# A mixture-of-experts layer behind an attention block: experts' outputs scaled on leaving PSUM and summed in DRAM by accumulating scatters, the tail's weights streamed as a 33rd expert

## The reference

```
xt = rms_norm(h, ffn_norm)
top_vals, top_idx = top_k(xt @ w_router + b_router, 4); gates = softmax(top_vals)
for expert e, for its tokens:
  y = ((clip(xt @ w_up[e] + b_up[e]) + 1) * swish(min(xt @ w_gate[e] + b_gate[e], 7))) @ w_down[e] + b_down[e]
h = h + sum over a token's 4 experts of gate * y
gate = sigmoid(rms_norm(h, ple_gate_norm) @ w_ple_gate)          # 1024 x 1024
e    = rms_norm(p @ w_ple_proj, ple_post_norm)                   # p: 512 x 256
h    = h + gate * e
```

## Time and profile before

| | |
|---|---|
| median of 3 runs | 2425.62 us |
| the profiled execution | 2424.97 us, its span 2423.1 us |
| mean granted clock of TensorE | 0.932 |
| PE, DVE, ACT, POOL busy | 90%, 65%, 55%, 10% |
| first product of the first expert | at 1137.2 us |
| last product of the last expert | done at 2290.5 us |
| tail | 2290.5 to 2423.1 us |

### The profile page before, as it was taken

The page is one execution under the profiler, slowest core; times in us unless marked ns, Lnnn a source line. Parts: engine busy times, 40 slices in busy tenths (PEclk is TensorE's granted clock), DMA queues, the critical chain, the costliest instruction groups (busy, mean ns, idle before and its releaser), DMA issues.

```text
span 2423.1 us, 31445 instructions
## 1 busy us (share of the span) xinstructions
PE 2171.8 (90%) x10638; PEld 1792.3 (74%) x10638; DVE 1564.7 (65%) x1788; ACT 1333.8 (55%) x1692; POOL 232.9 (10%) x168
## 2 busy tenths in 40 slices
PE   4985797899989597986999999999999999999828
PEld 3874675788868586775888888888888888888617
DVE  3314772222232436557988988988898898898753
ACT  2213452222222423314888888888888888888722
POOL 0000000000000000002111211211221121121220
PEclk9987798999999897697999999999999999999969
DMA  3334002122322221032999999999999999999850
GB/s 132 105 140 155 30 1 78 61 100 92 104 70 87 96 70 57 1 116 108 404 377 381 383 374 380 378 384 381 378 381 380 377 384 377 378 384 378 331 199 35
DMA packets 91167, 546.88 MB, mean 226 GB/s; under 512 B 13317, under 2 KB 15961, under 8 KB 32986
## 3 DMA queue, kind: packets, MB, share of 16 engines
q1 hardware_dynamic: 71744, 493.90, 54.1%
q10 hardware_dynamic: 12154, 25.84, 2.9%
q0 software_dynamic: 7200, 26.22, 2.7%
HBM read 514.98 MB, written 29.36 MB: 225 GB/s over the span
## 4 chain that ended last, share of the span: by engine, by line
PE 86%; DVE 7%; DMA 2%; ACT 2%; issue 2%; ACTq 0%; POOL 0%; POOLq 0%; DVEq 0%; SPq 0%
PE PS L1953 15%; PE PS L1955 14%; PE PS L1954 14%; PE PS L233 10%; PE PS L235 10%; PE PS L234 10%; PE PS L1950 2%; PE PS L922 2%; PE PS L307 2%; PE PS L1871 1%; PE PS L1963 1%; PE PS L1351 1%; DMA RING<-c_oh 1%; PE PS L990 1%; DVE X L2252 1%
## 5 line engine op out<-in xcount | busy, mean ns | idle before, releaser
L1865 DVE TENSOR_TENSOR WL<-RING,WH 128x2048 fp32r<-128x2048 f32 x388 | 879.5, 2287 | 111.1 <-ACT WH L1861 107.7
L1861 ACT ACTIVATE WH<-RING 128x1024 fp32r<-128x1024 f32 x776 | 807.9, 1058 | 174.8 <-PE PS L1955 165.5
L1953 PE MATMUL PS<-WH,RA 128*128 128x512 f32 x1540 | 639.1, 415 | 0.0
L1955 PE MATMUL PS<-WH,RA 128*128 128x512 f32 x1540 | 600.9, 390 | 0.0
L1954 PE MATMUL PS<-WL,RA 128*128 128x512 f32 x1540 | 600.2, 390 | 0.0
L229 DVE TENSOR_TENSOR WL<-RING,WH 128x2048 fp32r<-128x2048 f32 (+2 forms) x60 | 133.4, 2224 | 480.6 <-ACT WH L221 480.6
L221 ACT ACTIVATE WH<-RING 128x2048 fp32r<-128x2048 f32 (+2 forms) x60 | 111.6, 1860 | 477.3 <-PE PS L235 445.9
L1955 PEld LDWEIGHTS PS<-WH,RA 128*128 128x128 f32 x1540 | 289.4, 188 | 62.8
L1954 PEld LDWEIGHTS PS<-WL,RA 128*128 128x128 f32 x1540 | 290.1, 188 | 58.9
L1953 PEld LDWEIGHTS PS<-WH,RA 128*128 128x128 f32 x1540 | 291.2, 189 | 54.5
L233 PE MATMUL PS<-WH,RA 128*128 128x512 f32 (+2 forms) x640 | 246.1, 385 | 45.3 <-DVE RA L322 30.8
(11 more groups left out here) (330 smaller groups left out, 2285.0 us busy)
## 6 DMA issues: line engine op xcount, KB each, us to landing
RING<-w_experts SPq DMA_DIRECT2D x390, 1024.0 KB, 7.2
RING<-w_front SPq DMA_DIRECT2D x60, 1024.0 KB, 4.9
y_scr<-AR ACTq DMA_DIRECT2D x32, 512.0 KB, 8.9
y_scr<-AR SPq DMA_DIRECT2D x16, 512.0 KB, 5.1
RING<-w_tail SPq DMA_DIRECT2D x4, 1024.0 KB, 6.4
X<-x SPq DMA_DIRECT2D x4, 512.0 KB, 5.6
xs_scr<-AR ACTq DMA_DIRECT2D x4, 512.0 KB, 3.4
out<-X SPq DMA_DIRECT2D x4, 512.0 KB, 2.6
```

The source lines that it names most:

```text
L1861: e.activation(WH[:, m % 3, v], RING[:, m % 6, v], ACT.Copy).then_inc(s("m_hi"), 1)
L1865: e.tensor_tensor(WL[:, m % 3, :], RING[:, m % 6, :], WH[:, m % 3, :].bitcast(F32), ALU.subtract).then_inc(s("m_lo"), 1)
L1953: e.matmul(PS[bank][:, :], lhs[0][:, kr + k, :], WH[:, m % 3, c], start=False, stop=False)
L1955: x = e.matmul(PS[bank][:, :], lhs[1][:, kr + k, :], WH[:, m % 3, c], start=False, stop=(stop and k == 3))
```

## The change

1. **Lists.** Empty slots now name token 768, and gathers and scatters run with a bounds check of 511, which leaves such rows out. A second list, `GLIST`, holds each slot's gate. It is made by the same kind of matmul, with the gates cut into three bfloat16 parts (`GB`) and multiplied into the one-hot matrices by POOL (`OHG`, `BLM`: six multiplications). The 32 list matmuls (16 for `GLIST`, 16 for the overflow blocks) move from the end of the routing to behind the first expert's first product (`pe_late_lists`).
2. **Order.** The splits of the first expert's pieces 1 and 2 move on ACT and DVE from behind the routing to within it. `SLOTN` moves behind the low part of the first expert's rows (`XL`).
3. **Experts.** ACT scales by the column `GCOL` while it copies from PSUM; `YY` is added into `acc_scr` (a copy of `X` in DRAM, stored by SP during the routing) by an indirect DMA from POOL's queue that accumulates. POOL copies the two columns for it (`GCOL`, `TCOL`) once the scatter before has landed; ACT waits for them.
4. **Tail.** `w_experts` has a 33rd expert with the tail's weights, which the last expert's prefetch loads; three of its pieces are also split within the loop. `g_moe` is raised twice, first without the wait for the last scatter. `X` is read back from `acc_scr`, the gathers and the 16 additions are gone. TensorE transposes `X` unscaled, in 32 transposes, and the scale is applied in the sigmoid; the result is stored in eight halves.
5. `y_scr`, its filling with zeros and the waits for it are gone.

The DMA of `c_iot` into `RE4` only raises `d_y` to its first 16. The core of the diff:

```diff
-            e.wait_ge(s("v_win"), AT["v_gm"] + 8)
-            e.memset(ZERO, 0.0).then_inc(s("g_zero"), 1)
-
-        def sp_zero(e):
-            e.wait_ge(s("g_zero"), 1)
-            for b in range(NOV):
-                e.dma_start(y_d[(NE + b) * 128:(NE + b + 1) * 128, :], ZERO).then_inc(s("d_zero"), 16)
...
                 sp_expert_load(e, n, n, 0)
+
+            for i in range(4):
+                e.wait_ge(s("v_x"), 20 + i + 1)
+                e.dma_start(acc_d[i * 128:(i + 1) * 128, :], X[:, i, :]).then_inc(s("d_acc"), 16)
...
+
+        def pe_late_lists(e):
+
             for i in range(4):
                 for k in range(4):
-                    x = e.matmul(PS[3][:, 128:144], SLOTN[:, i, k, :], BLO[:, i, k, :], start=(i == 0 and k == 0),
+                    if i == 0 and k == 0:
+                        e.wait_ge(s("g_ohg"), 3)
+                    x = e.matmul(PS[4][:, 0:96], SLOT1[i][:, k, :], OHG[:, 4 * i + k, :, :], start=(i == 0 and k == 0), stop=(i == 3 and k == 3))
+            x.then_inc(s("p_rt"), 1)
+            e.wait_ge(s("v_route"), AT["v_blm"] + 1)
+            e.wait_ge(s("g_blm"), 3)
+            for i in range(4):
+                e.wait_ge(s("v_slot"), i + 1)
+                for k in range(4):
+                    x = e.matmul(PS[5][:, 0:80], SLOTN[:, i, k, :], BLM[:, i, k, :, :], start=(i == 0 and k == 0),
                                  stop=(i == 3 and k == 3))
             x.then_inc(s("p_rt"), 1)
 
...
+            e.wait_ge(s("p_pr"), CH[62].done)
+            act_expert_split(e, 1, 16, None)
             rows_put(0, 0, 0)
...
+            e.wait_ge(s("p_pr"), CH[63].done)
+            act_expert_split(e, 2, 16, None)
             for i in range(4):
...
             places(0)
+            dve_expert_split(e, 1, 4)
             best(2)
             places(1)
+            dve_expert_split(e, 2, 6)
...
-            e.tensor_scalar(LIST[:, 0:32], PS[7][:, 0:32], 256.0, None, ALU.add).then_inc(s("v_route"), 1)
+
+            e.tensor_scalar(LTMP, PS[7][:, 32:64], -512.0, 768.0, ALU.mult, ALU.add).then_inc(v_c.sem, v_c.up())
+            e.wait_ge(v_c.sem, v_c.n)
+            e.tensor_tensor(LIST[:, 0:32], LTMP, PS[7][:, 0:32], ALU.add).then_inc(s("v_route"), 1)
...
+            e.tensor_copy(GB[:, 0, :], fl(GK)).then_inc(v_c.sem, v_c.up())
+            e.wait_ge(v_c.sem, v_c.n)
+            e.tensor_tensor(GR1, fl(GK), GB[:, 0, :], ALU.subtract).then_inc(v_c.sem, v_c.up())
+            e.wait_ge(v_c.sem, v_c.n)
+            e.tensor_copy(GB[:, 1, :], GR1).then_inc(v_c.sem, v_c.up())
+            e.wait_ge(v_c.sem, v_c.n)
+            e.tensor_tensor(GB[:, 2, :], GR1, GB[:, 1, :], ALU.subtract).then_inc(s("v_route"), 1)
             dve_steps(e, QK, POSK, TMK, (128.0, 256.0, 384.0)).then_inc(v_c.sem, v_c.up())
...
-                e.tensor_tensor(BLT, mid(IOT16, 4), bc(TMK[:, i, :], 16), ALU.is_equal).then_inc(v_c.sem, v_c.up())
...
-                x = e.tensor_tensor(SLOTN[:, i], mid(IOT, 4), bc(PMK[:, i, :], 128), ALU.is_equal)
+                e.tensor_tensor(BLM[:, i, :, 1, :], mid(IOT16, 4), bc(TMK[:, i, :], 16), ALU.is_equal).then_inc(v_c.sem, v_c.up())
...
+                x = e.tensor_scalar(BLM[:, i, :, 0, :], BLM[:, i, :, 1, :], TOKF[:, i:i + 1], None, ALU.mult)
-            e.tensor_copy(DSTI, DST).then_inc(v_c.sem, v_c.up())
...
-            e.tensor_tensor(GKEEP, GK, bc(GS, 4), ALU.mult).then_inc(v_c.sem, v_c.up())
-            dve_expert_split(e, 1, 4)
-            e.wait_ge(s("p_rt"), 4)
-            e.tensor_scalar(LIST[:, 32:48], PS[3][:, 128:144], 256.0, None, ALU.add).then_inc(s("v_route"), 1)
...
-            for n in range(2, 4):
-                dve_expert_split(e, n, 2 * n + 2)
+            for i in range(4):
+                e.tensor_tensor(SLOTN[:, i], mid(IOT, 4), bc(PMK[:, i, :], 128), ALU.is_equal).then_inc(s("v_slot"), 1)
+            e.wait_ge(s("p_rt"), 4)
+            e.tensor_copy(GLIST[:, 0:32], PS[4][:, 0:32]).then_inc(v_c.sem, v_c.up())
+            for v in (1, 2):
+                e.wait_ge(v_c.sem, v_c.n)
+                e.tensor_tensor(GLIST[:, 0:32], GLIST[:, 0:32], PS[4][:, 32 * v:32 * v + 32], ALU.add).then_inc(v_c.sem, v_c.up())
+            e.wait_ge(s("p_rt"), 5)
...
+            e.tensor_tensor(LIST[:, 32:48], LTMP[:, 0:16], PS[5][:, 0:16], ALU.add).then_inc(s("v_route"), 1)
+            dve_expert_split(e, 3, 8)
 
         def pe_experts_start(e):
...
+        def pool_gather(e, tokens):
+
+            e.indirect_dma_start(XG, None, xs_d, bass.IndirectOffsetOnAxis(tokens, 0), bounds_check=511, oob_is_err=False
+                                 ).then_inc(s("d_xg"), 16)
 
         def pool_experts_start(e):
             e.sem_inc(s("g_sel"), 1)
             e.sem_inc(s("g_sed"), 1)
             e.wait_ge(s("v_route"), AT["v_li"] + 1)
             e.wait_ge(s("d_xs"), 64)
-            e.indirect_dma_start(XG, None, xs_d, bass.IndirectOffsetOnAxis(LIST[:, 0:1], 0)).then_inc(s("d_xg"), 16)
+            pool_gather(e, LIST[:, 0:1])
+
+            e.dma_start(RE4, A["c_iot"][:, 0:4]).then_inc(s("d_y"), 16)
+            for v in range(3):
+                if v == 0:
+                    e.wait_ge(s("v_route"), AT["v_g3"] + 1)
+                e.tensor_tensor(OHG[:, :, v, :], OHK.rearrange("p i k e -> p (i k) e"), bc(GB[:, v, :], 32), ALU.mult
+                                ).then_inc(s("g_ohg"), 1)
+            e.wait_ge(s("v_route"), AT["v_blm"] + 1)
+            for v in range(3):
+                e.tensor_tensor(BLM.rearrange("p i k v n -> p (i k) v n")[:, :, 2 + v, :],
+                                BLM.rearrange("p i k v n -> p (i k) v n")[:, :, 1, :], bc(GB[:, v, :], 16), ALU.mult
+                                ).then_inc(s("g_blm"), 1)
             e.wait_ge(s("p_xg"), 2)
-            e.indirect_dma_start(XG, None, xs_d, bass.IndirectOffsetOnAxis(LIST[:, 1:2], 0)).then_inc(s("d_xg"), 16)
+            pool_gather(e, LIST[:, 1:2])
             e.wait_ge(s("v_selb"), 2)
+            e.wait_ge(s("d_acc"), 64)
             e.wait_ge(s("v_route"), AT["v_dst"] + 1)
...
             e.wait_ge(s("d_y"), it * 16 + (b * 16 + 16))
-            e.activation(YY[:, 0:512], PS[4][:, :], ACT.Copy).then_inc(s("a_yy"), 1)
+            e.wait_ge(s("g_col"), it * 2 + (b * 2 + 2))
+            e.activation(YY[:, 0:512], PS[4][:, :], ACT.Copy, scale=GCOL).then_inc(s("a_yy"), 1)
             split(15)
             e.wait_ge(s("p_mm"), it * 24 + (b * 24 + 26 + MM_LEAD))
-            e.activation(YY[:, 512:1024], PS[5][:, :], ACT.Copy).then_inc(s("a_yy"), 1)
-            e.wait_ge(s("a_yy"), it * 2 + (b * 2 + 4))
-            e.dma_start(y_d[bass.ds((it + b) * 128, 128), :], YY).then_inc(s("d_y"), 16)
+            e.activation(YY[:, 512:1024], PS[5][:, :], ACT.Copy, scale=GCOL).then_inc(s("a_yy"), 1)
 
...
+            e.wait_ge(s("d_y"), it * 16 + (b * 16 + 16))
+            e.sem_inc(s("settle_pool"), 1)
+            e.tensor_copy(GCOL, GLIST[:, bass.ds(it + b, 1)]).then_inc(s("g_col"), 1)
+            e.tensor_copy(TCOL, LIST[:, bass.ds(it + b, 1)]).then_inc(s("g_col"), 1)
+            e.wait_ge(s("a_yy"), it * 2 + (b * 2 + 4))
+            e.sem_inc(s("settle_pool"), 1)
+            e.wait_ge(s("g_col"), it * 2 + (b * 2 + 2))
+            e.sem_inc(s("settle_pool"), 1)
+            e.indirect_dma_start(acc_d, bass.IndirectOffsetOnAxis(TCOL, 0), YY, None, bounds_check=511, oob_is_err=False,
+                                 compute_op=ALU.add).then_inc(s("d_y"), 16)
...
             e.sem_inc(s("g_moe"), 1)
+            e.wait_ge(s("d_y"), nn * 16 + (NE * 16 + 16))
+            e.sem_inc(s("settle_pool"), 1)
+            e.sem_inc(s("g_moe"), 1)
...
+            e.wait_ge(s("g_moe"), 2)
+            for i in range(4):
+                e.dma_start(X[:, i, :], acc_d[i * 128:(i + 1) * 128, :]).then_inc(s(f"d_x{i}"), 16)
+            for half in range(2):
+                for i in range(4):
+                    e.wait_ge(s("v_out"), 4 * half + i + 1)
+                    e.dma_start(A["out"][0, i * 128:(i + 1) * 128, 512 * half:512 * half + 512], X[:, i, 512 * half:512 * half + 512]
+                                ).then_inc(s("d_out"), 16)
+            e.wait_ge(s("d_out"), 128)
...
-            for n in range(16):
-                if n >= 8:
-                    e.wait_ge(s("v_add"), n - 7)
-                e.indirect_dma_start(YG[n % 8], None, y_d, bass.IndirectOffsetOnAxis(DSTI[:, n // 4, n % 4:n % 4 + 1], 0)
-                                     ).then_inc(s(f"d_yg{n % 8}"), 16)
...
+            e.wait_ge(s("v_xt"), XT["emb"] + 2)
+            e.wait_ge(s("g_moe"), 1)
+            for n in range(8):
+                i, half = n // 2, n % 2
+                if n >= 4:
+                    e.wait_ge(s("v_emb"), n - 3)
+                for k in range(2):
+                    c = slice(1024 * k + 512 * half, 1024 * k + 512 * half + 512)
```

(112 more changed lines are left out.)

221 lines of the change are left out of this document (70 added, 151 removed).

## The result

| | before | changed |
|---|---|---|
| times in the same measurement, us | 2424.56, 2425.62, 2426.24, 2427.24 | 2344.97, 2345.44, 2346.34, 2367.30 |
| median, us | 2425.93 | 2345.89 |
| profiled execution, its span, its clock | 2424.97, 2423.1, 0.932 | 2344.97, 2343.0, 0.953 |

One run of the changed kernel lies apart, at 2367.3 us and with a mean clock of 0.943. The experiments show that each kernel has two groups of times some 20 us apart, early and late, by when TensorE's clock comes back in the second block's attention; all four runs of before in the table are late ones.

A forecast was written before the change was run, and what follows sets the result against it. The prediction took TensorE to bound the experts, DVE the routing's end and waits the tail. Its sum was 2424.97 - 61.6 + 5.1 = 2368.5 us, 2369 on the median's scale, range 2358 to 2388.

The forecast's parts named there:

- the ground of the sum: Whole kernel: the profiled execution of before, 2424.97 us, to which the predicted gains and losses were added.
- Experts, 0 us: Expert loop: TensorE is the bound at 35.90 us an expert, so moving other engines' work changes nothing, 0 us.
- Routing, +5.1 us: Routing up to the loop's entry: four terms sum to +5.1 us, between -2.2 and +12.4.
- Ahead of the list: Routing: two splits put ahead of the first list make DVE reach it later, +4.0 us, bounds +0.9 and +6.6.
- List to `XL`: Routing, first list to low part of rows: work leaves, contention with POOL costs +3.5, together -0.8 us (-4.3 to +1.2).
- The list products and the loop's entry: First expert's start: 32 list matmuls after the first product, +1.4 us, and ACT's wait for `LIST`'s last columns, +0.5.
- Tail, -61.6 us: Last product to end: projection starts beside the last scatter, gathers and additions go, -61.6 us; end at 2361.5, bounds 2358 and 2375.
- A: Tail: the last scatter is late, `X` comes 11.5 us after the projection's end, 2380 us; chance 0.11.
- B: Start of the experts: POOL and DVE hold each other up, routing at its upper bounds, 2376 us; chance 0.10.
- D: Whole kernel: everything meets its lower bound, collisions vanish and the clock holds, 2358 us or below; chance 0.04.
- E: Tail: its weight pieces aren't there in time, the projection waits one load more, 7.2 us, giving 2376; chance 0.03.
- C: Experts: the accumulating scatter slows every expert; kernel slower from 29 us landing on, 2524 us at 32; chance 0.04.

The follow-up runs named there:

- experiment 1: Changed kernel with the zero fill put back, into a DRAM tensor nobody reads: four runs at 2345.0 to 2347.0 us, two at 2366.1 and 2366.9.
- experiment 9: Changed kernel with the first expert's two weight splits put back behind the routing: two runs at 2345.0 and 2345.1 us, four at 2365.5 to 2368.3.
- experiment 10: Changed kernel with POOL's six products of one-hots by gates held behind the first expert's tokens: 2344.6 and 2345.5 us, 2365.3 and 2367.8.
- experiment 7: Changed kernel with every expert's scatter issued twice, the second after the first has landed: 2356.6 and 2358.7 us, 2381.2 and 2381.9.

## Why the prediction was wrong

**The step that failed** is the ground of the sum, 2424.97 us, and with it a term that the sum doesn't have: everything ahead of the routing stands in it at 0 us, and the only reason given is that no wait ended on the zero fill. The front does hold no edit that matters (experiment 1), but the profiled execution and all three runs shown had met the late return of the clock, and I took that as part of the kernel. The changed kernel's profiled run came out of that stage 21.7 us ahead, with the clock back at 971 us instead of 1017. The stretches of before gave reason to ask: over 60 us at clock 0.50 with TensorE busy all the while. The range needed a case for "the clock comes back early", at 2369 - 21.7 = 2347 us, with a chance near one half by the later counts. The late run of the changed kernel took 2367.3 us, beside the forecast of 2369; which group the median fell in was chance. Group against group the sum was 2 to 4 us too pessimistic. What decides between the early and the late return stays open.

**Experts, 0 us:** right. 35.90 us, `GCOL` six us early, a scatter of 10.6 us against 25 to spare. (The prediction says 27; POOL asks for the landing 25.2 us after it issued the scatter, at 2059.96 and 2049.30 + 35.90.)

**Routing, +5.1 us:** measured +3.8. Ahead of the list +4.2 for +4.0, confirmed by experiment 9. List to `XL` -2.1 for -0.8: the contention with POOL is there (experiment 10), at 2.4 us rather than 3.5. The list products and the loop's entry +1.7 for +1.9.

**Tail, -61.6 us:** measured -62.2. The projection starts 5.2 us after the last product, reckoned 5.8: the scatter keeps POOL 2.18 us, not 0.97, but the flag follows its issue at once. The projection 12.8 us for 12.4, with the clock at 0.69 over its first stretch; transposes and gate 47.8 for 47.6; the end 4.6 for 5.2. The last scatter landed in 6.7 us instead of 5 and stayed hidden.

```profile
2277.00:2281.00 4.00, 3.17 (x9) 2.53 (x10) 0.28 (x2) 0.69 (x2) 0.54 (x1) 0.69 0.66 93
```

**Rivals:** A, B, D and E did not come. C did not either, but its cause shows at twice the traffic (experiment 7), as the passage of the Trainium skill named beside it has it (DMA: Bandwidth & Descriptors, "Issuing engines are not separate DMA queues"): the weights land in 11.9 us instead of 7.2. That passage gives no size, and with one scatter an expert nothing is lost. The rule named for the routing (the Trainium skill, SBUF — State Buffer, "Who interferes with whom") fits experiment 10 for two of the three long steps, which have two inputs; the third, a `TENSOR_SCALAR` with one, took 0.96 us as well, and the rule as the prediction gives it doesn't cover that.
